# An fp32 transformer encoder on one core: layer 0's last expert added to x by products instead of a scatter

## The chip, the cores and the metric

The program runs on one core of a Trainium2 chip. The metric is the device time of one execution in microseconds (us), the median over runs. Five engines have instruction streams of their own and meet only at semaphores: TensorE (PE, matrix products into PSUM), VectorE (DVE), ScalarE (ACT), GpSimd (POOL) and SyncE (SP, which here only issues DMAs). An engine's instructions run in the order in which they are written.

## What is computed

Two request groups (256 prompt tokens and 512 sample tokens, 768 rows of 1024 numbers in all) pass through two layers. Each layer is an attention mixer and then an expert layer:

```python
for i in range(DEPTH):
    h = rms_norm(x, norm_mix[i])
    x = x + (dilated_attention(h, ...) if i % 2 == 0 else local_gqa_attention(h, ...))
    h = rms_norm(x, norm_ffn[i])
    x = x + expert_choice_ffn(h, moe_router[i], moe_w_gate[i], moe_w_up[i], moe_w_down[i])

def expert_choice_ffn(h, w_router, w_gate, w_up, w_down):
    affinity = softmax(tokens @ w_router)            # 16 experts
    gate, idx = top_k(affinity.T, cap)               # each expert takes its best tokens
    xe = tokens[idx]
    hid = silu(xe @ w_gate) * (xe @ w_up)
    ye = (hid @ w_down) * gate[..., None]
    return zeros_like(tokens).at[idx].add(ye)
```

An expert takes 64 sample tokens and 32 prompt tokens: 96 slots. All is in fp32.

## The kernel before

The 768 rows are six tiles of 128 rows. `x` in SBUF holds them. Weight products are split by hand: a weight tile `w` becomes `w_hi` (rounded, written by ScalarE) and `w_lo = w - w_hi` (VectorE), the rows likewise, and three products of the fast reduced type replace one fp32 product. In the expert layer a piece of 256 weight rows (1 MB) is loaded by SP into a ring of six, split by ScalarE and VectorE and used by TensorE. `PIECE` is the order of the 192 pieces of a layer; gate, up and down of 16 experts.

`y[:, e % 2]` holds the weighted output of expert `e` (`take_y`, ScalarE). The POOL function `add_rows` scatters it by an indirect DMA that adds to the rows of the DRAM tensor `x_d` at the expert's tokens (`take[:, e]`); each scatter waits for the one before (`rows_added`). `x_d` was stored from `x` ahead of the experts.

**The boundary between the layers.** When expert 15's scatter has landed, SP loads the six tiles of `x` back from `x_d` (line 613); ahead of that it has issued the loads of the first two attention weight chunks (`load_chunk`, line 547), as soon as the last piece is used. Layer 1 then begins, with one order per engine, written out by hand:

- ScalarE: `high_chunk(first)` (the rounded half of the first weight chunk, line 789), then `sum_of_squares` of tiles 0 and 1 (line 762), then for each tile `take_transposed` (the rounded half of the transposed rows, line 771) with the sum of squares of the tile two ahead, and `take_tile` (the product out of PSUM, line 796) of the tile before. After tile 1's it makes the rounded half of the second chunk.
- VectorE: `low_chunk(first)` (line 1082), `row_means` (line 1096), then for each tile `scale_row` (line 1101: the row times its inverse norm times the gain), `row_means` of the next tile and `low_rows` (line 1088, the low half of the transposed rows) of the tile before; after tile 3's `low_rows(2)` the low half of the second chunk.
- POOL: the inverse root of each tile's mean square (line 694), one small instruction per tile.
- TensorE: sixty `idle_products` (line 1441, a 128x128 product of the identity whose result nobody reads), then `turn_rows`: for each tile eight transposes (line 1453), and behind them `project` of the tile before (lines 1487 to 1489, 24 products with the first weight chunk). `project` of tile t waits for `low_rows(t)`.

The loop in which TensorE runs through the tiles ends as follows:

```python
for t in range(NT):
    pe.wait_ge(h_ready, n + 1)
    ...                       # eight transposes of tile t
    if then is not None and t >= 1:
        then(t - 1)           # project(first, [t - 1])
```

Here "tile t's product" means these 24 instructions. Below, `first` is `FIRST_CHUNK[1]`.

Of the kernel before, what the change touches and what calls it, by code (L numbers as in the profile page):

```python
# [36 lines left out]
ALU = mybir.AluOpType  # L37
AX = mybir.AxisListType

P = 128  # L40
BANK = 512
DM = 1024
# [5 lines left out]
LAYERS = 2  # L48
# [62 lines left out]
def shape_constants():  # L111

    buckets = np.zeros((BUCKETS + 1, TABW), np.float32)
    for start, width, half, stride, every in TAB.values():
        for i in range(width):
            rel = i - (BAND - P - 1 if width > 2 * P else P - 1)
            if rel % every == 0 and abs(rel) // every <= half:
                buckets[t5_bucket(np.array(rel * stride)), start + i] = 1.0
            else:
                buckets[BUCKETS, start + i] = MASKED  # L120
    return {"c_buckets": buckets, "c_ident": np.eye(P, dtype=np.float32)}

# [39 lines left out]
def build_trunk(nc, d, outs):  # L162

    ctx = ExitStack()
    with ctx:
        def sb(name, shape, dt=F32, scope=ctx):
            return scope.enter_context(nc.sbuf_tensor(name, shape, dt))
# [37 lines left out]
        weight = sb("weight", [C, NE])  # L205
        take = sb("take", [C, NE], I32)
        take_s = sb("take_s", [CS, NE], I32)
        take_p = sb("take_p", [CP, NE], I32)
# [128 lines left out]
        weight_ready = sem("weight_ready")  # L337

        piece_in = [sem(f"piece_in{i}") for i in range(RAW)]
        hi_split = sem("hi_split")  # L340
# [18 lines left out]

        STREAM = [slice(PT_, NT), slice(0, PT_)]  # L360

        def down_bank(e):
# [177 lines left out]
        def _(sp):  # L540
# [61 lines left out]
            for layer in range(LAYERS):  # L602
                first = FIRST_CHUNK[layer]
                chunk = first
                if layer == 0:
                    chunk = 4
                else:
                    load_chunk(first)
                    load_chunk(first + 1)
                    chunk = first + 2  # L610
                    sp.wait_ge(rows_added, 16 * NE)
                    for t in range(NT):
                        sp.dma_start(x[:, t, :], x_d[t * P:(t + 1) * P, :]).then_inc(x_in[t], 16)
                load_bias(layer, 0)
                load_bias(layer, 1)
# [61 lines left out]
                if layer + 1 < LAYERS:  # L677
                    sp.dma_start(gain[:], bass.AP(d["norm_mix"].tensor, (layer + 1) * DM, [[0, P], [1, DM]])).then_inc(gain_in, 16)
                for n in range(layer * LAYER_PIECES + SPLIT, (layer + 1) * LAYER_PIECES):
                    load_piece(n)  # L680
            sp.wait_ge(x_out, 16 * NT * LAYERS)
            sp.wait_ge(rows_added, 16 * NE * LAYERS)
            sp.wait_ge(prompt_added, 16 * NE)
# [3 lines left out]
        def _(pool):  # L687
            hnorms = 0
            for layer in range(LAYERS):
# [21 lines left out]
                def add_rows(e):  # L711

                    n = layer * NE + e
                    pool.wait_ge(y_ready, n + 1)
                    if e == 0:
# [27 lines left out]
        def _(act):  # L743
            turned = 0
            lots = 0
            for layer in range(LAYERS):
                def sum_of_squares(step, i):
# [7 lines left out]
                    else:  # L755
                        act.wait_ge(x_in[t], 16 * (layer + 1))
                        scratch = ps[:, 4:6, :].rearrange("p b n -> p (b n)")
                    if n >= 1:
# [38 lines left out]

                if layer == 0:
                    sum_of_squares(0, 0)
                    sum_of_squares(0, 1)  # L800
                high_chunk(FIRST_CHUNK[layer])
                if layer:
                    sum_of_squares(2 * layer, 0)
                    sum_of_squares(2 * layer, 1)

# [219 lines left out]
                def take_y(e, n):  # L1025
# [3 lines left out]
                    if u >= 2:  # L1029
                        act.wait_ge(rows_added, 16 * (u - 1))  # L1030
                    if layer and e >= 2:
# [30 lines left out]
        def _(dve):  # L1062
# [13 lines left out]
            for layer in range(LAYERS):  # L1076
# [25 lines left out]


                gains += 1
                if layer:
                    low_chunk(FIRST_CHUNK[layer])
                row_means(2 * layer, 0)
                row_means(2 * layer, 1)
                dve.wait_ge(gain_in, 16 * gains)
                for t in range(NT):  # L1110
                    if t >= 2:
                        dve.wait_ge(h_turned, NT * 2 * layer + t - 1)
                    scale_row(2 * layer, t, t, rows[:, t % 2, :])
                    if t == 1 and layer == 0:
                        low_chunk(FIRST_CHUNK[layer])
# [268 lines left out]
                nc.vector.tensor_copy(take_s[:], ps[0:CS, 5, 0:NE])  # L1384
                nc.vector.tensor_copy(take_p[:], ps[0:CP, 5, 32:48])
                nc.vector.tensor_copy(weight[0:CS, :], ps[0:CS, 5, 64:64 + NE])
                nc.vector.tensor_copy(weight[CS:C, :], ps[CS:C, 5, 96:96 + NE]).then_inc(weight_ready, 1)
# [27 lines left out]
                for i, (kind, e, part) in enumerate(PIECE):  # L1415
# [11 lines left out]
                    if i + SPLIT < LAYER_PIECES:  # L1427
                        split(n + SPLIT)


        @block.tensor
        def _(pe):
# [5 lines left out]
            def idle_products(count, bank=6):  # L1438

                for i in range(count):  # L1440
                    nc.tensor.matmul(ps[:, bank, 0:P], ident[:], ident[:], start=True, stop=True)  # L1441

            for layer in range(LAYERS):
                def turn_rows(s, src, then=None):
                    for t in range(NT):
                        n = NT * s + t
                        pe.wait_ge(h_ready, n + 1)
# [45 lines left out]
                if layer:  # L1493
                    idle_products(60)
                turn_rows(2 * layer, lambda t: rows[:, t % 2, :], lambda t: project(FIRST_CHUNK[layer], [t]))
# [341 lines left out]
```

## Time and profile before

| | us |
|---|---|
| median of 3 runs | 1850.18 |
| lowest and highest of them | 1849.69, 1852.94 |
| the profiled execution's own time | 1845.36 |
| its span, first to last instruction | 1843.5 |
| TensorE busy in the span | 1766.0 (96%) |
| VectorE, ScalarE, POOL busy | 1330.8, 1132.1, 238.4 |
| TensorE's share of the chain that ended last | 88% |

All times inside the trace count from the start of the span. The profiled execution is one of its own, 4.8 us below the median of the runs, so differences are worked out against it. The boundary between the layers lies at 946 us. The experts of layer 0 fill 390 to 946 us, those of layer 1 begin at 1276 us.

### The profile page before, as it was taken

What the parts mean: (1) busy time and instruction counts of PE and PEld (TensorE: products, weight loads), DVE (VectorE), ACT (ScalarE), POOL (GpSimd) and SP (SyncE); (2) the same over time, 40 slices, a digit from 0 to 9 for tenths busy, and PEclk for the clock granted to TensorE, in tenths of its full rate; (3) what the DMA queues carried; (4) which work ended last, traced back from release to release, by engine and by line L of the source; (5) the groups of instructions that cost most, each with busy time, mean ns of one, the idle gap of its engine ahead of it and who ended that gap; (6) DMA issues with size and microseconds to landing.
All of it is one profiled execution on the core that took longest, in us unless ns stands there. A gap on an engine that the chain in (4) does not pass through costs nothing.

```text
span 1843.5 us, 24587 instructions
## 1 busy us (share of the span) xinstructions
PE 1766.0 (96%) x10322; PEld 1393.7 (76%) x10322; DVE 1330.8 (72%) x1008; ACT 1132.1 (61%) x1185; POOL 238.4 (13%) x118
## 2 busy tenths in 40 slices
PE   6989999989999999999999989998999999999997
PEld 6878889977776776776779977997767767777775
DVE  4634455578888888888845556557888888888885
ACT  4344443357777777777743556434777777777774
POOL 0201000000010010010011100001111311311311
PEclk9999998999999999999999989999999999999999
DMA  4401113399999999999954012229999999999994
GB/s 159 113 30 53 44 51 108 144 354 370 389 376 384 391 380 383 394 382 383 390 181 105 18 36 56 80 97 344 361 382 392 380 384 389 375 384 393 382 389 142
DMA packets 155842, 486.00 MB, mean 264 GB/s; under 512 B 12200, under 2 KB 46120, under 8 KB 155688
## 3 DMA queue, kind: packets, MB, share of 16 engines
q1 hardware_dynamic: 148308, 459.26, 66.6%
q0 software_dynamic: 7424, 25.17, 5.8%
q8 instruction: 82, 1.34, 0.3%
q14 instruction: 28, 0.22, 0.0%
HBM read 454.26 MB, written 30.13 MB: 263 GB/s over the span
## 4 chain that ended last, share of the span: by engine, by line
PE 88%; DVE 5%; ACT 3%; DMA 2%; issue 1%; POOL 1%; SPq 0%; POOLq 0%; DVEq 0%; ACTq 0%
PE ps L1789 19%; PE ps L1791 19%; PE ps L1790 19%; PE ps L1487 5%; PE ps L1488 4%; PE ps L1489 4%; PE ps L1567 2%; PE ps L1679 2%; PE ps L1681 2%; PE ps L1680 2%; PE ps L1760 1%; PE ps L1539 1%; PE ps L1441 1%; PE ps L1753 1%; PE ps L1556 1%
## 5 line engine op out<-in xcount | busy, mean ns | idle before, releaser
L1296 DVE TENSOR_TENSOR w_lo<-ring,w_hi 128x2048 fp32r<-128x2048 f32 x384 | 876.7, 2290 | 153.1 <-ACT w_hi L1001 152.9
L1001 ACT ACTIVATE w_hi<-ring 128x2048 fp32r<-128x2048 f32 x384 | 735.9, 1917 | 276.7 <-PE ps L1791 268.4
L1789 PE MATMUL ps<-w_hi,xe_hi 128*96 128x512 f32 x1016 | 403.5, 397 | 0.0
L1791 PE MATMUL ps<-w_hi,xe_lo 128*96 128x512 f32 x1016 | 399.2, 393 | 0.0
L1790 PE MATMUL ps<-w_lo,xe_hi 128*96 128x512 f32 x1016 | 398.1, 392 | 0.0
L1791 PEld LDWEIGHTS ps<-w_hi,xe_lo 128*96 128x96 f32 x1016 | 163.9, 161 | 71.5
L1789 PEld LDWEIGHTS ps<-w_hi,xe_hi 128*96 128x96 f32 x1016 | 163.7, 161 | 69.5 <-DVE xe_lo L1395 5.6
L1790 PEld LDWEIGHTS ps<-w_lo,xe_hi 128*96 128x96 f32 x1016 | 164.3, 162 | 64.5
L1789 PE MATMUL ps<-w_hi,hid_hi 128*96 128x512 f32 x512 | 201.6, 394 | 0.0
L1791 PE MATMUL ps<-w_hi,hid_lo 128*96 128x512 f32 x512 | 201.1, 393 | 0.0
L1487 PE MATMUL ps<-c_hi,hT_hi 128*128 128x256 f32 x648 | 191.4, 295 | 9.6 <-issue 3.4
L1790 PE MATMUL ps<-w_lo,hid_hi 128*96 128x512 f32 x512 | 200.3, 391 | 0.0
L1488 PE MATMUL ps<-c_lo,hT_hi 128*128 128x256 f32 x648 | 186.9, 288 | 0.0
L1489 PE MATMUL ps<-c_hi,hT_lo 128*128 128x256 f32 x648 | 186.7, 288 | 0.0
L1487 PEld LDWEIGHTS ps<-c_hi,hT_hi 128*128 128x128 f32 x648 | 128.1, 198 | 16.0 <-issue 14.8
L1488 PEld LDWEIGHTS ps<-c_lo,hT_hi 128*128 128x128 f32 x648 | 128.4, 198 | 0.0
L1489 PEld LDWEIGHTS ps<-c_hi,hT_lo 128*128 128x128 f32 x648 | 128.3, 198 | 0.0
L1791 PEld LDWEIGHTS ps<-w_hi,hid_lo 128*96 128x96 f32 x512 | 82.5, 161 | 36.1
L1790 PEld LDWEIGHTS ps<-w_lo,hid_hi 128*96 128x96 f32 x512 | 82.7, 162 | 35.6
L1789 PEld LDWEIGHTS ps<-w_hi,hid_hi 128*96 128x96 f32 x512 | 82.5, 161 | 34.9
L720 POOL DMA_INDIRECT layer_rows<-y,take x16 | 36.8, 2302 | 492.1 <-ACT y L1034 492.1
L1237 DVE SCALAR_TENSOR_TENSOR probs<-ps,bias 128x512 f32<-128x512 f32 (+2 forms) x30 | 34.6, 1153 | 89.3 <-PE ps L1539 89.3
(190 smaller groups left out, 2255.1 us busy)
## 6 DMA issues: line engine op xcount, KB each, us to landing
ring<-in_moe_w_gate SPq DMA_DIRECT2D x128, 1024.0 KB, 7.2
ring<-in_moe_w_up SPq DMA_DIRECT2D x128, 1024.0 KB, 8.5
ring<-in_moe_w_down SPq DMA_DIRECT2D x128, 1024.0 KB, 8.6
wbuf<-in_a_w_in SPq DMA_DIRECT2D x9, 1024.0 KB, 5.5
ffn_rows<-hrow SPq DMA_DIRECT2D x12, 512.0 KB, 2.7
wbuf<-in_b_w_in SPq DMA_DIRECT2D x5, 1024.0 KB, 8.2
unit_rows<-row SPq DMA_DIRECT2D x36, 132.0 KB, 1.8
bias<-bias_rows SPq DMA_DIRECT2D x4, 768.0 KB, 10.1
```

Source lines behind the costliest of these rows:

```text
L1001: nc.scalar.activation(w_hi[:, n % SPLIT], ring[:, n % RAW], ACT.Copy).then_inc(hi_split, 1)
L1296: nc.vector.tensor_tensor(w_lo[:, n % SPLIT], ring[:, n % RAW], w_hi[:, n % SPLIT].bitcast(F32), ALU.subtract).then_inc(lo_split, 1)
L1487: nc.tensor.matmul(out, hi, c_hi[:, w, k, :], start=(k == (KM - 1 if folding else 0)), stop=False)
L1488: nc.tensor.matmul(out, hi, c_lo[:, w, k, :], start=False, stop=False)
L1489: ins = nc.tensor.matmul(out, lo, c_hi[:, w, k, :], start=False, stop=(k == (0 if folding else KM - 1)))
L1567: ins = nc.tensor.matmul(u_bank[:, h * HD:(h + 1) * HD], probsT[:, (lots + i) % 2, m * P:(m + 1) * P], v[:, g % 2 if layer == 0 else 0, k, ...
L1679: nc.tensor.matmul(out, hi, of_hi[:, k, :], start=(k == 0), stop=False)
L1680: nc.tensor.matmul(out, hi, of_lo[:, k, :], start=False, stop=False)
L1681: ins = nc.tensor.matmul(out, lo, of_hi[:, k, :], start=False, stop=(k == KX - 1))
L1789: nc.tensor.matmul(out, hi[:, k, :], w_hi[:, n % SPLIT, i, cols], start=(k == 0), stop=False)
L1790: nc.tensor.matmul(out, hi[:, k, :], w_lo[:, n % SPLIT, i, cols], start=False, stop=False)
L1791: ins = nc.tensor.matmul(out, lo[:, k, :], w_hi[:, n % SPLIT, i, cols], start=False, stop=(k == KM - 1))
```

## The change

Expert 15 of layer 0 is scattered no more. A row of the numbers 0 to 767 (`c_tokens`) is loaded during layer 0's experts, and VectorE compares it with the token of each of the expert's 96 slots (`last_slot`): `slot_tokens` is a matrix of 96 x 768 with a 1 where a slot holds a token. For each tile TensorE multiplies 128 columns of it with `y` (96 x 1024) in two fp32 products of 512 columns (`last_expert`), and VectorE adds the two PSUM banks to the tile of `x` (`add_last`). SP loads `x` when expert 14's scatter has landed; the first weight chunk is loaded behind tile 1, the second behind tile 5. The sums of squares of the first two tiles go ahead of the first chunk's rounded half, VectorE's `low_chunk(first)` goes behind `scale_row(1)`, and 14 idle products stand where 60 stood. The products of tiles 0 to 3 stand ahead of these, those of tiles 4 and 5 inside `turn_rows`.

```diff
+        slot_tokens = hrow[0:C, NT - 1, 0:TOK]
+        token_row = x[0:C, 0, 0:TOK]
+        LAST_BANK = (4, 2, 4, 2, 4, 4)
+        def rows_before(layer, e):
+            return e if layer == 0 else NE - 1 + e
...
-                    load_chunk(first)
-                    load_chunk(first + 1)
                     chunk = first + 2
-                    sp.wait_ge(rows_added, 16 * NE)
+                    sp.wait_ge(slots_marked, 1)
+                    sp.wait_ge(rows_added, 16 * (NE - 1))
                     for t in range(NT):
                         sp.dma_start(x[:, t, :], x_d[t * P:(t + 1) * P, :]).then_inc(x_in[t], 16)
+                        if t == 1:
+                            load_chunk(first)
+                    load_chunk(first + 1)
...
                 for n in range(layer * LAYER_PIECES + SPLIT, (layer + 1) * LAYER_PIECES):
+                    if layer == 0 and n == LAYER_PIECES // 2:
+                        sp.wait_ge(weight_ready, 1)
+                        sp.wait_ge(x_out, 16 * NT)
+                        sp.dma_start(token_row, bass.AP(d["c_tokens"].tensor, 0, [[0, C], [1, TOK]])).then_inc(tokens_in, 16)
                     load_piece(n)
...
+                    n = rows_before(layer, e)
+                    if layer == 0 and e == NE - 1:
+                        return
...
-                        act.wait_ge(x_in[t], 16 * (layer + 1))
-                        scratch = ps[:, 4:6, :].rearrange("p b n -> p (b n)")
+                        if layer:
+                            act.wait_ge(last_added, t + 1)
+                            scratch = qraw[:, :, :].rearrange("p t c -> p (t c)")[:, 0:DM]
...
-                if layer == 0:
-                    sum_of_squares(0, 0)
-                    sum_of_squares(0, 1)
+                sum_of_squares(2 * layer, 0)
+                sum_of_squares(2 * layer, 1)
                 high_chunk(FIRST_CHUNK[layer])
-                if layer:
-                    sum_of_squares(2 * layer, 0)
-                    sum_of_squares(2 * layer, 1)
...
+                def add_last(t):
+                    dve.wait_ge(x_in[t], 32)
+                    dve.wait_ge(last_rows, t + 1)
+                    b = LAST_BANK[t]
+                    nc.vector.tensor_tensor(x[:, t, :], ps[:, b:b + 2, :].rearrange("p b n -> p (b n)"), x[:, t, :],
+                                            ALU.add).then_inc(last_added, 1)
                 if layer:
-                    low_chunk(FIRST_CHUNK[layer])
+                    add_last(0)
+                    add_last(1)
                 row_means(2 * layer, 0)
+                if layer:
+                    add_last(2)
                 row_means(2 * layer, 1)
...
                     scale_row(2 * layer, t, t, rows[:, t % 2, :])
-                    if t == 1 and layer == 0:
+                    if layer and t + 3 < NT:
+                        add_last(t + 3)
+                    if t == 1:
                         low_chunk(FIRST_CHUNK[layer])
                     if 1 <= t < NT - 1:
                         row_means(2 * layer, t + 1)
                     if t >= 1:
                         low_rows(t - 1)
...
+                if layer == 0:
+                    nc.vector.tensor_scalar(last_slot[0:CS, :], ps[0:CS, 5, NE - 1:NE], float(SEQ), None, ALU.add)
+                    nc.vector.tensor_copy(last_slot[CS:C, :], ps[CS:C, 5, 32 + NE - 1:32 + NE])
...
+                    if layer == 0 and kind == "down" and part == 0 and e == NE - 3:
+                        dve.wait_ge(tokens_in, 16)
+                        nc.vector.tensor_scalar(slot_tokens, token_row, last_slot[:], None, ALU.is_equal).then_inc(slots_marked, 1)
...
+            def last_expert(t):
+                if t == 0:
+                    pe.wait_ge(slots_marked, 1)
+                if t >= 2:
+                    pe.wait_ge(last_added, t - 1 if t < NT - 1 else t)
+                for half in range(2):
+                    ins = nc.tensor.matmul(ps[:, LAST_BANK[t] + half, :], slot_tokens[:, t * P:(t + 1) * P],
+                                           y[:, (NE - 1) % 2, half * BANK:(half + 1) * BANK], start=True, stop=True)
+                ins.then_inc(last_rows, 1)
...
                     for t in range(NT):
+                        if s == 2 and 1 <= t < NT - 3:
+                            last_expert(t + 3)
...
                 if layer:
-                    idle_products(60)
+                    for t in range(4):
+                        last_expert(t)
+                    idle_products(14)
```

## Rows read from the trace of the kernel before

**Rows 1.** Chain of waits at the layer boundary: start us, length us, what.

```profile
946.08 1.12 ACT y L1034
...
947.46 8.34 DMA layer_rows<-y,take
955.82 0.34 SPq L613
956.21 4.60 DMA x<-layer_rows
...
963.83 1.30 DVE v L1101
...
970.70 0.87 PE ps L1453 x8
...
974.77 1.91 ACT c_hi L789
...
978.91 1.28 DVE v L1101
...
981.53 0.36 PE ps L1487
```

**Rows 2.** Timeline of TensorE: start, length, line, shapes, count, idle before.

```profile
947.24 13.66 PE L1441 MATMUL ps<-ident 128*128 128x128 f32 x120 [1.20 <-ACT y L1034]
...
967.00 0.55 PE L1487 MATMUL ps<-c_hi,hT_hi 128*128 128x256 f32 x1
...
971.33 0.36 PE L1487 MATMUL ps<-c_hi,hT_hi 128*128 128x256 f32 x1
...
974.29 1.03 PE L1453 MATMUL ps<-ident,v 128*128 128x128 f32 x8
```

**Rows 3.** Timelines of POOL, SyncE and VectorE, columns as above.

```profile
938.25 2.35 POOL L720 DMA_INDIRECT layer_rows<-y,take  x1 [44.37 <-ACT y L1034]
...
946.13 0.99 SPq L547 DMA_DIRECT2D wbuf<-in_b_w_in  x2
...
968.23 1.23 DVE L1088 TENSOR_TENSOR hT_lo<-ps,hT_hi 128x1024 fp32r<-128x1024 f32 x1
...
976.70 2.29 DVE L1082 TENSOR_TENSOR c_lo<-wbuf,c_hi 128x2048 fp32r<-128x2048 f32 x1 [2.37 <-ACT c_hi L789]
```

**Rows 4.** Issue to landing: expert 14's scatter, the six x loads, weight loads.

```profile
DMA to landing us min/median/max: 6.4/6.4/6.4
...
DMA to landing us min/median/max: 3.7/5.8/7.6
...
DMA to landing us min/median/max: 5.5/9.4/10.7
```

**Rows 5.** Instructions by line: fp32 products of 512 columns, the add from PSUM.

```profile
44.45 3.60 PE L1499 MATMUL ps<-bias,row 33*12 33x512 f32 x8
...
L1499 PE MATMUL ps<-bias,row x8: 589/589/597, 44.5 to 47.5; 33*12 33x512 f32 x8
...
L1284 DVE TENSOR_TENSOR x<-ps,x x12: 1224/1225/1226, 301.6 to 1248.0; 128x1024 f32<-128x1024 f32 x12
```

**Rows 6.** Windows of 1 us: busy time by engine, PEclk, DMA share, GB/s.

```profile
965.00:966.00 1.00, 0.83 (x4) 0.84 (x5) 0.55 (x3) 1.00 (x2) 0.55 (x1) 0.50 1.05 327
...
968.00:969.00 1.00, 1.00 (x9) 1.00 (x9) 0.88 (x3) 0.20 (x1) 0.55 (x1) 0.82 0.98 131
978.00:979.00 1.00, 0.20 (x2) 0.00 (x0) 1.00 (x2) 0.90 (x2) 0.00 (x0) 1.00 0.00 0
982.00:983.00 1.00, 1.00 (x8) 1.00 (x7) 1.00 (x2) 0.40 (x1) 0.00 (x0) 0.50 0.00 0
```

**Rows 7.** Who waits for whom in layer 0's experts; first gather before them.

```profile
ACT w_hi L1001 <- PE ps L1791: 133.2, 155, 1.5
DVE w_lo L1296 <- ACT w_hi L1001: 72.4, 138, 1.8
...
388.20 0.85 PE L1753 MATMUL ps<-ident,xg 96*128 96x96 f32 x8 [0.74 <-DMA xg<-ffn_rows,take]
```

More of the change, by code:

```diff
@@ L120, in shape_constants @@
                 buckets[BUCKETS, start + i] = MASKED
-    return {"c_buckets": buckets, "c_ident": np.eye(P, dtype=np.float32)}
+    return {"c_buckets": buckets, "c_ident": np.eye(P, dtype=np.float32),
+            "c_tokens": np.arange(TOK, dtype=np.float32)[None, :]}
 def units_of(layer):
@@ L206, in build_trunk @@
         take = sb("take", [C, NE], I32)
+        last_slot = sb("last_slot", [C, 1])
         take_s = sb("take_s", [CS, NE], I32)
@@ L337, in build_trunk @@
         weight_ready = sem("weight_ready")
+        tokens_in = sem("tokens_in")
+        slots_marked = sem("slots_marked")
+        last_rows = sem("last_rows")
+        last_added = sem("last_added")
         piece_in = [sem(f"piece_in{i}") for i in range(RAW)]
@@ L679, in _ @@
                 for n in range(layer * LAYER_PIECES + SPLIT, (layer + 1) * LAYER_PIECES):
+                    if layer == 0 and n == LAYER_PIECES // 2:
+                        sp.wait_ge(weight_ready, 1)
+                        sp.wait_ge(x_out, 16 * NT)
+                        sp.dma_start(token_row, bass.AP(d["c_tokens"].tensor, 0, [[0, C], [1, TOK]])).then_inc(tokens_in, 16)
                     load_piece(n)
             sp.wait_ge(x_out, 16 * NT * LAYERS)
-            sp.wait_ge(rows_added, 16 * NE * LAYERS)
+            sp.wait_ge(rows_added, 16 * rows_before(1, NE))
             sp.wait_ge(prompt_added, 16 * NE)
@@ L711, in add_rows @@
                 def add_rows(e):
-                    n = layer * NE + e
-                    pool.wait_ge(y_ready, n + 1)
+                    n = rows_before(layer, e)
+                    if layer == 0 and e == NE - 1:
+                        return
+                    pool.wait_ge(y_ready, layer * NE + e + 1)
                     if e == 0:
@@ L755, in sum_of_squares @@
                     else:
-                        act.wait_ge(x_in[t], 16 * (layer + 1))
-                        scratch = ps[:, 4:6, :].rearrange("p b n -> p (b n)")
+                        if layer:
+                            act.wait_ge(last_added, t + 1)
+                            scratch = qraw[:, :, :].rearrange("p t c -> p (t c)")[:, 0:DM]
+                        else:
+                            act.wait_ge(x_in[t], 16)
+                            scratch = ps[:, 4:6, :].rearrange("p b n -> p (b n)")
                     if n >= 1:
@@ L1029, in take_y @@
                     if u >= 2:
-                        act.wait_ge(rows_added, 16 * (u - 1))
+                        act.wait_ge(rows_added, 16 * (rows_before(layer, max(e - 1, 0))))
                     if layer and e >= 2:
```

## The prediction

> **What bounds the kernel now.** I read the page's engine shares first, then the chain of waits, then the engines' timelines around the one place that the change touches. TensorE is busy for 96% of the span and carries 88% of the chain. In layer 0's experts ScalarE waits for TensorE to free a split buffer, 133.2 us in total and never for a load, and VectorE for ScalarE [rows 7]: TensorE sets the pace there, and the other engines and the loads have room. At 946 us the chain leaves TensorE: ScalarE takes expert 15's output, the scatter needs 8.34 us, the reload of x 4.60 us from issue to the second tile, then sums, inverse roots and scaling [rows 1]. TensorE meanwhile runs its 60 idle products, 13.66 us [rows 2], transposes tile 0 at 963.4 and starts tile 0's product at 967.0. A second detour follows: tile 1's product ends at 974.29 [rows 2], ScalarE then makes the second chunk's rounded half, VectorE its low half, and only behind that scales tile 4, so that tile 3's product starts at 981.53 [rows 1]. From there to 1010 us TensorE is the chain, so what counts is how much earlier or later tile 3's product starts.
>
> **What can be had.** Expert 14's scatter was issued at 938.25 [rows 3] and landed 6.4 us later [rows 4], at 944.65, ahead of the last product. So the reload need not wait for expert 15, and the 8.34 us of its scatter leave the path. In exchange come twelve fp32 products, six adds and the first chunk's low half, which was hidden behind the scatter. I follow the new order engine by engine; a wait costs 0.05 us.
>
> **Step 1, the products of tiles 0 to 3.** The nearest rows of an fp32 product of 512 columns are line 1499's: each product is recorded as two, eight take 3.60 us and one alone 0.589, so a further one costs (3.60 - 0.59) / 7 = 0.43 us [rows 5]. A tile (two products, four records) costs 1.72 us, and 0.16 more until VectorE may read. The first starts when y is there, at 947.24, as the idle products did [rows 2]. x tile 0, issued at 944.7, lands 3.7 us later [rows 4], at 948.4. The six tiles landed between 959.5 (955.8 + 3.7) and 965.9 (958.3 + 7.6), one each 1.27 us, so tile 1 lands at 949.6. Both adds, 1.225 us each [rows 5], are done at 950.4 and 952.1, just ahead of the products of tiles 2 and 3 that reuse their banks. So TensorE runs through: 947.24 + 4 x 1.72 = 954.1. Fourteen idle products at 13.66 / 60 = 0.228 us bring it to 957.3.
>
> **Step 2, the first transposes.** The first chunk is issued at 946.13 as before [rows 3] but lies behind tiles 0 and 1; with 2.5 to 3 us for its 1 MB at the rate of x it lands at 952.5, and tiles 2 to 5 at 954.0, 955.3, 956.6 and 957.9. Add 2 ends at 955.3, tile 1's mean follows, and tile 0 is scaled (1.28 us) by 956.6. That is 0.7 us ahead of the end of the idle products: the transposes start at 957.3 instead of 963.4. 6.1 us are gained here.
>
> **Step 3, what is given back before tile 0's product.** Transposes 0.87 us [rows 1], to 958.2. Then TensorE has tile 4's products: to 959.9, readable at 960.1. VectorE has added tile 3 and scaled tile 1 by 958.9 and waits for them: add 4 to 961.3, then the first chunk's low half, 2.29 us [rows 3], to 963.6, then tile 0's low rows, 1.23 us [rows 3], to 964.8. Tile 0's product starts at 964.85 instead of 967.0: 2.15 us are left.
>
> **Step 4, the clock.** In the kernel before TensorE idled from 960.9 to 963.4, and the granted clock was 0.50 (1.2 GHz) from about 965 until some way into the 968 window, where it reads 0.82 [rows 6]: 3.3 us. The next idle stretch, 978.2 to 980.25, brought 0.50 at 982 [rows 6]. Now TensorE idles from 960.9 to 964.85, longer than either. I charge the stretch of about 3.2 us at 0.50 that both rows show, beginning with the product: 1.6 us of work are lost. At full clock a tile's product takes 24 x 0.12 = 2.9 us (971.33 to 974.29 with its hand-over [rows 2]), so it ends at 969.4.
>
> **Step 5, tile 5 stands in front of tile 1's product.** TensorE's order is now tile 0's product, tile 5's products, transposes 2, tile 1's product. Tile 5's are readable at 969.4 + 1.72 + 0.16 = 971.2. VectorE scaled tile 2 by 966.1 and stands at add 5 since; queued behind it are tile 3's mean and tile 1's low rows, for which tile 1's product waits. Add 5 ends at 972.4, the low rows at 973.7. In the kernel before these low rows were made at 968.23 [rows 3] and nobody waited. Tile 1's product starts at 973.75 instead of 971.33: 2.4 us later.
>
> **Step 6, the rest of the path.** The second detour hangs on the end of tile 1's product and moves with it: ScalarE's rounded half at 977.1 instead of 974.77, VectorE's low half (2.29 us), tile 4's scaling, transposes, tile 3's low rows; tile 3's product starts at 983.8 instead of 981.53. With the same idle stretch in front of it comes the same half clock behind it. Sum: 1.7 + 0.2 (tile 5's products) + 1.2 (its add) + 1.2 (the low rows behind it) + 0.2 of waits, less 2.15 gained, and 0.0 from the clock since tile 0's product loses what it lost before to within 0.3: between 2.2 and 2.4, I take **+2.3 us**. The same working on the old order gives 981.5 for tile 3's product, as the trace has it.
>
> **Edits costed at nothing.** The token row (0.3 MB) goes through SP's queue in the middle of the experts; ScalarE never waits for a piece there [rows 7], with weight loads of 1 MB landing in 5.5 to 10.7 us elsewhere [rows 4]; uncovered it would cost 0.8 us, its size at the rate of x. The comparison (96 x 768, bounded from above by the 1.225 us of a 1024-column add [rows 5]) falls into VectorE's waits for ScalarE, 72.4 us in 138 of them [rows 7]; uncovered 1.2 us, once. The two copies for `last_slot` delay the splits of the first pieces by 0.3 us while TensorE waits for the first gather until 388.20 [rows 7]. The missing scatter frees POOL, which is idle anyway. From below all these are nothing; none can gain.
>
> **Rivals.**
> *The clock falls once more, or for longer.* Step 5 opens a new idle stretch, 972.0 to 973.75, between the 1.2 us ahead of the idle products, after which these ran at their full rate [rows 2], and the 2.05 us that cost the clock [rows 6]. If it falls in tile 1's product, this ends 1.0 us later, tile 3's product starts 1.2 later, and what TensorE gains on its later half clock leaves +3.0; if the first low stretch covers all of tile 0's product, 1.1 us more: +4.1. [...] Chance 0.2.
> *x comes late: slower.* Tiles 2 to 5 lie behind a weight chunk now. One of the two chunks took 10.7 us to land [rows 4]; if the first does so here (956.8), tile 2 lands at 958.1 instead of 954.0. From 954.7 on each us of lateness is one of time: +5.7. Slower by over 0.2% from a landing of 956.1 on. For it speaks that six tiles and two chunks now share one stretch; against it that 10.7 belonged to the second chunk, beside a scatter. Chance 0.15, with expert 14's scatter needing more than 6.4 us.
> *The clock stays up: no loss.* If the dense products ahead keep it at full rate through both idle stretches, tile 0's product takes 2.9 us and tile 3's runs at full rate: 1.6 + 1.6 us less, **-0.9 us**. Against it stand both low stretches of before. To get past 0.2% faster it needs cheaper products too: at 0.23 us per record (the rate of the reduced products is the floor I allow) the sum would be -3.0. Chance 0.12.
>
> **How the numbers follow.** The sum stands against the profiled execution's 1845.36 us: 1847.7. The median of the runs is 4.8 us higher; the difference carries over, 1850.18 + 2.3 = 1852.5 us. 0.2%, about what a measurement of this kernel tells from no change, is 3.7 us. The sum has 0.53, with a range of its own from +0.7 to +3.6. Below it the range reaches to the case of -0.9, with 1.3 for the spread of runs: 1848.0; above to late x and the spread: 1857. Slower by over 0.2%: late x (0.15), half of the clock's case (0.1), a little of the sum: 0.27. Faster: 0.07 from the case of a full clock. Within 0.2%: 0.66.
>
> **What would show it.** Right: SP's first x load near 944.7; last idle product near 957; tile 0's product 2 us earlier, tile 1's 2 to 3 us later than before; VectorE's longest waits before adds 4 and 5, for TensorE; the low clock in tile 0's product. Wrong: tile 1's low rows done before tile 5's add; an add that waits for a load; records of the new products far from 0.43 us apart; PEclk at 1.00 throughout.

## The result and the profile after

The changed kernel is a little slower: its median is 1854.18 us in ten runs (1850.38 to 1857.8), beside 1849.19 us in ten runs of the kernel before (1844.2 to 1852.94). The ratio is 1.0028 with a 95% interval of 1.0017 to 1.0039: 5.2 us more, between 3.1 and 7.2. A second measurement (e7) gave 1.0023 (1.0014 to 1.0033), 4.3 us. The forecast was +2.3 us, 1852.5 (1848 to 1857). The sign and the place were right; the size was about half of what was measured. Times given as "measured" are medians; the ratios stand against the kernel before, run beside. One run of the twelve of experiment e8 took 7668.78 us and is left out of its figures.

The two profiled executions differ by about as much, 1850.38 against 1845.36 us, but for the most part not at the place of the change. I set marks: the start of ScalarE's instruction that takes expert 15's output `y`, and the start of the one that takes the product of the boundary's last tile, tile 5 (ScalarE's timelines, before and after):

```profile
992.80 0.38 ACT L796 ACTIVATE kraw<-ps 128x256 f32<-128x256 f32 x1 [2.50 <-PE ps L1489]
```

```profile
992.61 0.38 ACT L824 ACTIVATE kraw<-ps 128x256 f32<-128x256 f32 x1 [2.50 <-PE ps L1546]
```

`y` is taken at 946.08 and 944.76 us in these two traces. From mark to mark ("the boundary" from here on) the kernel before took 46.72 us and the changed one 47.85: of the 5.1 us between the spans 1.1 lie here. The eighteen units of layer 1's attention took 120.22 and then 124.04 us, though nothing was changed in them.

The chain of waits of the changed kernel at the boundary (start, length, what) answers to [rows 1].

```profile
944.76 1.12 ACT y L1058
945.93 7.13 PE ps L1494 x16
953.06 3.13 PE ps L1485 x28
956.18 1.01 PE ps L1510 x8
957.20 1.73 PE ps L1494 x4
959.02 1.22 DVE x L1133
960.25 2.20 DVE c_lo L1106
962.51 1.14 DVE hT_lo L1112
...
968.25 1.73 PE ps L1494 x4
970.08 1.23 DVE x L1133
971.36 1.14 DVE hT_lo L1112
...
976.06 1.92 ACT c_hi L817
...
980.21 1.28 DVE v L1125
```

The scatter and the reload of x are gone from the chain, as the change intends. In their place stand sixteen records of the new products (L1494), the idle products, then tile 4's products, their add (L1133), the first chunk's low half (L1106) and tile 0's low rows (L1112); later tile 5's products, their add and tile 1's low rows. The second detour, from ScalarE's `c_hi` at 976.06 on, stands as it was.

The timeline of VectorE (start, length, line, what, idle time before and who ended it), beside [rows 3]:

```profile
953.57 1.22 DVE L1133 TENSOR_TENSOR x<-ps,x 128x1024 f32<-128x1024 f32 x1 [2.55 <-DMA x<-layer_rows]
...
959.02 1.22 DVE L1133 TENSOR_TENSOR x<-ps,x 128x1024 f32<-128x1024 f32 x1 [0.65 <-PE ps L1494]
...
970.08 1.23 DVE L1133 TENSOR_TENSOR x<-ps,x 128x1024 f32<-128x1024 f32 x1 [5.24 <-PE ps L1494]
971.22 0.14 DVE L1120 TENSOR_SCALAR var<-sumsq 128x1 f32<-128x1 f32 x1
971.28 1.22 DVE L1112 TENSOR_TENSOR hT_lo<-ps,hT_hi 128x1024 fp32r<-128x1024 f32 x1
```

VectorE stands 5.24 us at the add of tile 5 for TensorE's products, with tile 1's low rows behind it. TensorE in turn stands for those low rows. Its timeline, beside [rows 2]:

```profile
945.93 7.13 PE L1494 MATMUL ps<-y,hrow 96*128 96x512 f32 x16 [1.20 <-ACT y L1058]
...
963.79 0.55 PE L1544 MATMUL ps<-c_hi,hT_hi 128*128 128x256 f32 x1 [4.00 <-DVE hT_lo L1112]
...
972.64 0.36 PE L1544 MATMUL ps<-c_hi,hT_hi 128*128 128x256 f32 x1 [1.79 <-DVE hT_lo L1112]
...
981.55 1.09 PE L1510 MATMUL ps<-ident,v 128*128 128x128 f32 x8 [2.06 <-DVE v L1125]
```

Both new idle stretches are there, 4.00 us ahead of tile 0's product and 1.79 us ahead of tile 1's, and the old one of 2.06 us ahead of tile 4's transposes, which stand in front of tile 3's product. The windows of 1 us (the number behind the five engines is PEclk, TensorE's granted clock) show one low stretch in this execution, that is one run of windows at 0.50, the lower of the clock's two levels, in tile 0's product, where [rows 6] have two:

```profile
963.00:964.00 1.00, 0.21 (x1) 0.24 (x2) 1.00 (x2) 0.00 (x0) 0.14 (x1) 0.72 1.18 141
964.00:965.00 1.00, 1.00 (x6) 1.00 (x7) 0.83 (x1) 0.00 (x0) 0.00 (x0) 0.50 0.86 129
...
966.00:967.00 1.00, 1.00 (x7) 1.00 (x6) 0.00 (x0) 0.00 (x0) 0.00 (x0) 0.57 0.95 131
967.00:968.00 1.00, 1.00 (x11) 1.00 (x10) 0.00 (x0) 0.00 (x0) 0.00 (x0) 1.00 0.88 101
...
983.00:984.00 1.00, 1.00 (x10) 1.00 (x10) 1.00 (x2) 0.70 (x1) 0.00 (x0) 1.00 0.00 0
```

### The profile page after: what moved, and what is told of

Its sections match the earlier page's. It is cut to its first block, busy times and chain, and to the rows that moved or that the text cites. A ratio compares the mean times of both kernels' runs of the same rounds, so it can differ in the third digit from the quotient of the medians.

```text
span 1848.6 us, 24468 instructions
## 1 busy us (share of the span) xinstructions
PE 1764.6 (95%) x10254; PEld 1385.7 (75%) x10254; DVE 1338.2 (72%) x1017; ACT 1132.3 (61%) x1185; POOL 237.2 (13%) x117
## 4 chain that ended last, share of the span: by engine, by line
PE 88%; DVE 5%; ACT 3%; DMA 2%; issue 1%; POOL 1%; SPq 0%; POOLq 0%; DVEq 0%; ACTq 0%
PE ps L1848 19%; PE ps L1850 19%; PE ps L1849 19%; PE ps L1544 5%; PE ps L1546 4%; PE ps L1545 4%; PE ps L1626 2%; PE ps L1738 2%; PE ps L1740 2%; PE ps L1739 2%; PE ps L1598 2%; PE ps L1819 1%; PE ps L1485 1%; PE ps L1812 1%; PE ps L1615 1%
```

## The experiments

e1 to e4 ran on one chip, e5 to e8 on a second, the four single runs e9 to e12 on a third. The medians of the kernel before were 1850.55 us (35 runs) on the first and 1848.75 us (34 runs) on the second.

### e1: the kernel before once more

No edit. The question is whether low clock in layer 1's attention belongs to the change.

> The kernel before once more, for the granted clock of its single runs and a second trace. Theory A: the change costs about 2.6 us at the layer boundary (tile 3's product 2.6 us later after expert 15's output), and the rest of the measured 5 us is stretches of half clock elsewhere that come and go between executions of either kernel: then the mean granted clock of these runs scatters from 0.980 to 0.988 as that of the changed kernel does, and the new trace has low stretches at places where the first had none. Theory B: the change itself brings low stretches to layer 1 (at 1131 us and ahead of layer 1's experts, 4.5 us in the first trace): then these runs stay near 0.988 and the new trace has full clock at both places.

Measured: 1848.92 us, ratio 0.999 (0.9977 to 1.0004); the profiled span was 1850.5 us, 7.0 us longer than the first trace of the very same kernel. Layer 1's attention took 125.27 us instead of 120.22. The windows that cover it exactly, first of the first trace, then of this one:

```profile
1054.85:1175.07 120.22, 109.66 (x841) 94.25 (x839) 67.49 (x70) 68.78 (x205) 8.33 (x2) 0.96 0.19 53
```

```profile
1055.20:1180.47 125.27, 113.06 (x841) 96.24 (x839) 67.55 (x70) 68.55 (x205) 8.33 (x2) 0.93 0.19 51
...
981.00:982.00 1.00, 1.00 (x7) 1.00 (x8) 1.00 (x1) 0.00 (x0) 0.55 (x1) 0.69 0.00 0
982.00:983.00 1.00, 1.00 (x6) 0.96 (x5) 1.00 (x2) 0.38 (x1) 0.00 (x0) 0.50 0.00 0
```

The same 841 matmul records run at a mean granted clock of 0.93 instead of 0.96, and TensorE is busy for 3.4 us longer with them. So what the two first traces differ by in layer 1 is no work of the change: the first trace of before was the luckiest of all fourteen there (the others took 121.9 to 126.6 us). Theory B falls; the mean granted clock of these runs, too, scatters from 0.981 to 0.989, as Theory A had it. The last two lines are from the boundary: this execution has only the second of the low stretches of [rows 6], at tile 3's product, and its boundary is 45.52 us, 1.2 shorter than in the first trace.

### e2: the preparations alone

The kernel before with the token row, `last_slot` and the comparison, whose result nobody uses:

```diff
+                        sp.dma_start(token_row, bass.AP(d["c_tokens"].tensor, 0, [[0, C], [1, TOK]])).then_inc(tokens_in, 16)
...
+                    nc.vector.tensor_scalar(last_slot[0:CS, :], ps[0:CS, 5, NE - 1:NE], float(SEQ), None, ALU.add)
+                    nc.vector.tensor_copy(last_slot[CS:C, :], ps[CS:C, 5, 32 + NE - 1:32 + NE])
...
+                        nc.vector.tensor_scalar(slot_tokens, token_row, last_slot[:], None, ALU.is_equal).then_inc(slots_marked, 1)
```

> The kernel before with layer 0's part of the change alone: token row, slot tokens and the comparison are made but not used; scatter, reload and layer 1 are as before. By the working in which these edits cost nothing: 0 us, within 1.5 us. Rival: they are the unexplained part of the loss, 2 to 3 us slower, with a TensorE wait near the comparison in expert 13 or ahead of the first gather.

Measured: 1851.48 us, ratio 0.9999 (0.9985 to 1.0012). From the first expert's output to the sixteenth's layer 0 took 508.16 us, beside 508.11 in the first trace of before. The comparison itself took 0.61 us and nobody waited for it (the instruction's own view):

```profile
L1447 DVE TENSOR_SCALAR hrow<-x,last_slot x1: 610/610/610, 883.6 to 883.6; 96x768 f32<-96x768 f32 x1
```

These edits cost nothing, as the forecast had it.

### e3: tile 5's products ahead of tile 1's transposes

Tile 5 gets banks of its own, so that its products can go directly behind tile 4's, ahead of tile 0's product:

```diff
-        LAST_BANK = (4, 2, 4, 2, 4, 4)
+        LAST_BANK = (4, 2, 4, 2, 6, 4)
...
-                    pe.wait_ge(last_added, t - 1 if t < NT - 1 else t)
+                    pe.wait_ge(last_added, min(t - 1, 3))
...
-                        if s == 2 and 1 <= t < NT - 3:
-                            last_expert(t + 3)
+                        if s == 2 and t == 1:
+                            last_expert(4)
+                            last_expert(5)
```

> The changed kernel with tile 4's products in banks 6 and 7 and tile 5's right behind them, ahead of tile 1's transposes, so that nothing stands between tile 0's and tile 1's product but the transposes of tile 2. If step 5 is what loses the gain: counted from expert 15's output, tile 0's product starts as in the changed kernel (19.0 us), tile 1's starts 24.5 us after it instead of 27.9 (26.6 in the kernel before was 25.25), and the time falls by 3.4 us against the changed kernel, to about 1 us below the kernel before by the boundary alone. If instead the clock or layer 0's edits make the loss, tile 1's product moves as said but the time stays 4 to 5 us above the kernel before.

(A bracket in this text is garbled: the start of tile 1's product in the kernel before, counted from `y`, is 971.33 - 946.08 = 25.25 us [rows 1, 2].)

Measured: 1849.78 us, ratio 0.9999 (0.9988 to 1.0009). The whole loss is gone. VectorE's timeline shows how:

```profile
964.79 1.22 DVE L1133 TENSOR_TENSOR x<-ps,x 128x1024 f32<-128x1024 f32 x1
...
965.99 1.21 DVE L1112 TENSOR_TENSOR hT_lo<-ps,hT_hi 128x1024 fp32r<-128x1024 f32 x1
...
974.38 2.29 DVE L1106 TENSOR_TENSOR c_lo<-wbuf,c_hi 128x2048 fp32r<-128x2048 f32 x1 [2.37 <-ACT c_hi L817]
```

The add of tile 5 waits for nobody, tile 1's low rows are done at 967.2, before tile 0's product ends, and tile 1's product is taken 27.76 us after `y` instead of 31.02 in the changed kernel. The boundary is 44.58 us, 3.3 us below the first trace of the changed kernel, which lost as much to the clock (table below); 3.4 us were expected. So step 5 is what eats the gain.

### e4: the first idle stretch filled

Seventeen idle products between tile 1's transposes and tile 0's product:

```diff
                        ins.then_inc(h_turned, 1)
+                        if s == 2 and t == 1:
+                            idle_products(17)
```

> The changed kernel with 17 idle products between tile 1's transposes and tile 0's product, where TensorE idled 4.0 us. If the low clock in tile 0's product comes from that gap: PEclk 1.00 there, the product takes 2.9 us instead of 4.4, and the time falls by 1.5 us against the changed kernel, still 2 to 3.5 us above the kernel before. If the low stretch has another cause, the product keeps its 4.4 us and the time does not change.

Measured: 1852.6 us, ratio 1.0014 (1.0002 to 1.0027). TensorE now waits for 0.20 us instead of 4.00, and the clock stays up (timeline, then two of the windows):

```profile
960.94 3.96 PE L1485 MATMUL ps<-ident 128*128 128x128 f32 x34
965.10 0.36 PE L1546 MATMUL ps<-c_hi,hT_hi 128*128 128x256 f32 x1 [0.20 <-DVE hT_lo L1112]
...
966.00:967.00 1.00, 1.00 (x11) 1.00 (x10) 0.15 (x1) 0.00 (x0) 0.00 (x0) 1.00 0.94 121
967.00:968.00 1.00, 1.00 (x11) 1.00 (x10) 0.00 (x0) 0.00 (x0) 0.00 (x0) 1.00 0.99 129
```

Tile 0's product is taken 22.02 us after `y` instead of 23.53: the 1.5 us that step 4 charged to the clock. Then a low stretch appears at tile 3's product, which the first trace of the changed kernel did not have, and the boundary comes out at 47.48. One portion of clock was saved, another was paid elsewhere; 1.79 us of waiting ahead of tile 1's product remain. The timed ratio, beside 1.0028 and 1.0023 of the changed kernel with overlapping intervals, is too coarse to show a gain of 1.5 us.

### e5: the reload alone, without the products

No products and no adds, so expert 15's rows of layer 0 are left out; 36 idle products keep TensorE busy instead:

```diff
-                            act.wait_ge(last_added, t + 1)
+                            act.wait_ge(x_in[t], 32)
...
                     dve.wait_ge(x_in[t], 32)
-                    dve.wait_ge(last_rows, t + 1)
...
+                    return
...
-                        if s == 2 and 1 <= t < NT - 3:
-                            last_expert(t + 3)
...
-                    for t in range(4):
-                        last_expert(t)
-                    idle_products(14)
+                    idle_products(36)
```

> The changed kernel without the twelve products and six adds (expert 15's rows of layer 0 are left out), 36 idle products in place of 14. It prices what the early load of x is worth when nothing has to be added. By the steps: counted from expert 15's output, tile 0's product starts at 12.6 us (kernel before 20.9, changed kernel 19.0), tile 5's product is taken at about 38 us (before 45.4 to 46.7, changed 47.9), and the time is 8 to 9 us below the kernel before: the products and adds then take back 10 us. Rival: the reload is not what bounds the boundary, and the time falls by less than 4 us.

Measured: 1844.6 us, ratio 0.9973 (0.9964 to 0.9982), 5.0 us (3.3 to 6.7) faster than before, not 8 to 9. The interval alone does not exclude the rival's 4 us; the boundary, 40.42 us, is 5.0 to 6.3 us shorter than in any trace of the kernel before. The trace shows where the rest went. The mean of tile 1 stands in VectorE's order behind tile 2's wait for x, which I had left in (VectorE's timeline, then TensorE's):

```profile
956.48 0.15 DVE L1120 TENSOR_SCALAR var<-sumsq 128x1 f32<-128x1 f32 x1 [6.24 <-DMA x<-layer_rows]
956.93 2.48 DVE L1125 SCALAR_TENSOR_TENSOR v<-x,rstd,gain 128x1024 f32<-128x1024 f32 x2 [0.29 <-issue]
...
958.27 3.45 PE L1505 MATMUL ps<-ident,v 128*128 128x128 f32 x16 [2.57 <-DVE v L1125]
```

Tile 2 landed 10.2 us after `y` (946.23 in this trace), beside 8.4 to 8.8 in the four traces of the changed kernel, where VectorE waits for it too, but TensorE's products and idle products last longer. TensorE idled for 2.57 us, the clock fell to 0.50 in the transposes (3.45 us for two tiles that take 2 x 0.87 at full clock), and tile 0's product started at 16.72 instead of 12.6. The miss is my wait and the late load. Why the load landed later here I can't say.

### e6: a new order

All that e3 showed, and the first chunk behind tile 2 of x. ScalarE's and VectorE's orders are written out (a: add of the last expert, m: mean, s: scaling, c: a chunk's half, l: low rows; q: sum of squares, h: taking a transposed tile, k: taking a product; the digit is the tile, or the chunk). Tile 0's product still waits for the fifth add:

```diff
+        LAST_BANK = (4, 2, 4, 2, 6, 4)
+        ACT_ORDER = order("q0 q1 c0 h0 q2 q3 h1 q4 k0 h2 k1 q5 h3 c1 h4 k2 k3 h5 k4 k5")
+        DVE_ORDER = order("a0 a1 m0 a2 m1 s0 s1 c0 a3 l0 a4 m2 l1 m3 m4 s2 s3 a5 l2 s4 m5 l3 s5 l4 c1 l5")
...
-                        if t == 1:
+                        if t == 2:
                             load_chunk(first)
...
+                        if s == 2 and t == 1:
+                            last_expert(4)
+                            last_expert(5)
+                            pe.wait_ge(last_added, 4)
...
+                        if s == 2 and t == 1:
+                            pe.wait_ge(last_added, 5)
...
-                    idle_products(14)
+                    idle_products(4)
```

> The change with another order in layer 1's first stretch: tiles 4 and 5 multiplied behind tile 0's transposes (banks 6 and 4), the first chunk loaded behind tile 2, rows of tiles 0 and 1 scaled ahead of the adds of tiles 3 to 5, low rows ahead of the adds that nobody waits for, the second chunk's halves made late. If the loss was only the order in which the adds and products stand: tile 0's product starts 16.0 us after expert 15's output (changed kernel 19.0, before 20.9), tile 1's 19.8 (27.9, 25.3), tile 5's is taken at 36.9 (47.9, 45.4 to 46.7), no low clock in between, and the time is 8 to 9 us below the kernel before. If the fp32 products themselves are too dear whatever their place: not below the kernel before by more than 3 us.

Measured: 1844.54 us, ratio 0.997 (0.9958 to 0.9983): by the ratio 5.5 us faster than the kernel before (by the medians 4.2), and by the medians 8.7 us faster than the changed kernel beside it (e7), the fastest of the kernels that leave nothing out. 8 to 9 us against the kernel before were expected. The boundary is 39.05 us. The rows show the third add, the start of tile 0's product and the transposes of tiles 4 and 5:

```profile
953.07 1.23 DVE L1154 TENSOR_TENSOR x<-ps,x 128x1024 f32<-128x1024 f32 x1 [0.43 <-PE ps L1525]
...
962.92 0.39 PE L1579 MATMUL ps<-c_hi,hT_hi 128*128 128x256 f32 x1 [1.17 <-DVE x L1154]
...
974.87 1.04 PE L1543 MATMUL ps<-ident,v 128*128 128x128 f32 x8
...
978.61 1.04 PE L1543 MATMUL ps<-ident,v 128*128 128x128 f32 x8
```

No add waits for a load, and tile 0's product starts 16.5 us after `y` (946.38) instead of 19.0. That is 0.5 us later than expected, and the product still ran through a low stretch (taken 4.67 us after its start, in e4 at full clock 3.14), so the boundary came out 2.1 us above the expected 36.9.

Not all of this undoes step 5. Of the 5.5 us between this boundary and e3's, 2.9 come ahead of tile 0's product (16.54 us after `y` against 19.43). Most of the rest is the second detour: the second chunk's halves are made late (c1), so TensorE no longer stands for 2 us ahead of tile 4's transposes. The kernel before has that detour too and could have been spared it; no run tried this, so what e6 gains over the kernel before is not the price of the change in a good order alone.

### e7: the changed kernel once more

No edit.

> The changed kernel once more, on the same chip as the others, for a second interval and a second trace. By the sum of steps 1 to 6: 2.3 us above the kernel before, with tile 5's product taken 47 to 49 us after expert 15's output. Rival (something outside the boundary adds to it): 4 us or more above, at the same boundary.

Measured: 1853.19 us, ratio 1.0023 (1.0014 to 1.0033). Its boundary took 49.73 us instead of 47.85. Both are above what was expected (2.3 us over the kernel before, a boundary of 47 to 49), and the rival does not fit either, as it kept the boundary as it was. The windows show a low stretch that begins ahead of tile 0's product and lasts through all of it, and later a second one:

```profile
964.00:965.00 1.00, 0.00 (x0) 0.00 (x0) 1.00 (x3) 0.00 (x0) 0.00 (x0) 0.62 0.97 144
...
970.00:971.00 1.00, 1.00 (x7) 1.00 (x6) 0.00 (x0) 0.00 (x0) 0.00 (x0) 0.50 0.94 141
971.00:972.00 1.00, 1.00 (x6) 0.71 (x5) 0.00 (x0) 0.48 (x2) 0.00 (x0) 0.97 0.72 91
...
985.00:986.00 1.00, 1.00 (x6) 1.00 (x6) 1.00 (x2) 0.00 (x0) 0.42 (x1) 0.50 0.00 0
```

### e8: the first chunk's low half ahead of the fourth add

```diff
+                    if t == (0 if layer else 1):
+                        low_chunk(FIRST_CHUNK[layer])
                     if layer and t + 3 < NT:
                         add_last(t + 3)
-                    if t == 1:
-                        low_chunk(FIRST_CHUNK[layer])
```

> The changed kernel with VectorE's low half of the first chunk moved ahead of tile 3's add, nothing else. It prices step 3's low half and leaves step 5 in place. By the working tile 0's product starts at 18.4 us after expert 15's output instead of 19.0, as the adds of tiles 3 and 4 now stand behind the low half; TensorE's idle stretch is cut in two of 2.0 and 1.5 us. If the clock then stays up, tile 1's product starts at 25.7 instead of 27.9 and the time falls by 2.1 us against the changed kernel; if not, by 0.6.

Measured: 1850.2 us, ratio 1.0013 (0.9999 to 1.0026), boundary 47.26. Tile 0's product starts 18.3 us after `y` and each product is taken 0.6 us earlier than in the first trace of the changed kernel; the clock falls as before. The timed difference to e7 (1.0023) is larger than 0.6 us, but the intervals overlap. The low half is a small part of the wait; the order of tile 5 is the large one.

### e9 to e12: four more traces, two of each kernel

No edits; e9 and e11 are the kernel before, e10 and e12 the changed one.

> One more trace of the kernel before. Where does the part of the loss sit that the boundary traces do not show (boundary +2.9 us in the mean, timed +4.1 and +4.7 us)? If in low clock at the boundary that differs from one execution to the next: from expert 15's output to tile 5's product 43.5 to 46.7 us here, so that the mean of the traces of before falls below 45.9. If it sits in layer 1's attention: 66 to 149 us later stages shorter here than in the changed kernel.

> As the other look at the kernel before: boundary 43.5 to 46.7 us, attention of layer 1 between 120 and 127 us.

> One more trace of the changed kernel: from expert 15's output to tile 5's product 47.9 to 49.7 us as in its two traces (before 45.4 to 46.7); the attention of layer 1 between 120 and 127 us as in every kernel. If the unexplained part is in the attention, this stretch is at its long end here each time.

> As the other look at the changed kernel: boundary 47.9 to 49.7 us, attention of layer 1 between 120 and 127 us.

Measured: 1851.84 and 1848.94 us for the kernel before, 1851.29 and 1853.35 for the changed one; one more run of the kernel before beside them took 1843.27, so single runs decide nothing. Their boundaries are what counts. With all earlier traces they make this table, whose second column adds up 1 - PEclk over the windows of 1 us from `y` to 52 us behind it: the full-speed work that the low clock took away.

| kernel, trace | boundary us | lost to the clock us |
|---|---|---|
| before, first trace | 46.72 | 3.4 |
| e1 | 45.52 | 1.7 |
| e2 (before with the preparations) | 45.39 | 1.7 |
| e9 | 45.58 | 1.7 |
| e11 | 46.34 | 3.4 |
| after, first trace | 47.85 | 1.7 |
| e7 | 49.73 | 5.1 |
| e10 | 50.65 | 5.1 |
| e12 | 49.62 | 5.1 |
| e3 tile 5 early | 44.58 | 1.7 |
| e4 gap filled | 47.48 | 1.7 |
| e8 chunk ahead | 47.26 | 1.7 |
| e5 no products | 40.42 | 1.7 |
| e6 new order | 39.05 | 1.7 |

In e10 the second of three low stretches lies in tile 1's product, right behind the new idle stretch of 1.79 us:

```profile
972.00:973.00 1.00, 0.37 (x3) 0.40 (x4) 1.00 (x2) 0.00 (x0) 0.00 (x0) 1.00 0.00 0
973.00:974.00 1.00, 1.00 (x10) 1.00 (x10) 1.00 (x3) 0.00 (x0) 0.18 (x1) 0.93 0.00 0
974.00:975.00 1.00, 1.00 (x7) 1.00 (x7) 0.87 (x1) 0.00 (x0) 0.36 (x1) 0.50 0.00 0
```

The five traces with the boundary of before have a mean of 45.91 us, the four of the changed kernel 49.46: +3.55 us, inside both timed intervals. Traces with the same loss to the clock, one portion of 1.7 us, give 47.85 against a mean of 45.50: **+2.35 us**, the forecast, though on the side of the changed kernel this is a single trace. The rest, 3.55 - 2.35 = 1.2 us, is by this count the clock: the four traces lost 4.3 us to it on average, the five 2.4, and part of that difference of 1.9 falls where TensorE idles anyway.

Two expectations are answered by this, one of them with a miss. The mean of the traces of before did not fall below 45.9; it is the changed kernel that came out longer, e10 with 50.65 us above the 47.9 to 49.7 that were expected. And the missing part does not sit in layer 1's attention, which took 121.97 and 123.69 us in e10 and e12, 125.26 and 123.32 in e9 and e11. Outside the boundary these nine traces show no loss on average: up to `y` the means are 946.3 us before and 945.7 after, behind tile 5's product 855.9 and 855.4.

## Why the prediction was right in its mechanism and too small in its size

**Step 1** held. Counted from `y`, everything came at the time forecast: sixteen records took 7.13 us, so 0.43 each with the first one's 0.59, and the last idle product ended 11.4 us after `y` (forecast 957.3 - 946.08 = 11.2). One part was off: tile 2 of x landed about 0.9 us later than forecast, VectorE's third add waited 2.55 us for it, and tile 0 was scaled at 956.04, only 0.15 us ahead of the idle products' end at 956.19. It cost nothing, by that little. "An add that waits for a load" was among the prediction's own signs of being wrong, and it came; and of VectorE's waits that were to be its longest, that ahead of add 4 was 0.65 us only.

**Step 2** held: the transposes began 11.4 us after `y` (11.2 forecast).

**Step 3** held: tile 0's product started 19.03 us after `y`, forecast 18.77, beside 20.92 before. 1.9 of the 2.15 us were left.

**Step 4** held in the first trace, with one low stretch in tile 0's product (taken at 23.53); e4, with the stretch gone, took it at 22.02, 1.5 us earlier, where 1.6 was charged. In e7 and e12 the low stretch was twice as long.

**Step 5** held, and e3 shows that it decides: tile 1's product started 27.88 us after `y` (forecast 27.67, before 25.25), VectorE waited 5.24 us at the add of tile 5, and with that add out of the way the loss was gone.

**Step 6** failed in one term, the "0.0 from the clock". The step took it that the changed kernel loses to the clock what the kernel before lost. It does in some executions and not on average: 1.7, 5.1, 5.1 and 5.1 us in four traces, beside 3.4, 1.7, 1.7, 1.7 and 3.4. The mechanical sum of the step, +2.3, came out at +2.35, so close with some luck, as it rests on one trace of the changed kernel; the clock added 1.2.

**The rivals.** *The clock falls once more, or for longer* is what most executions of the changed kernel do, and both of its forms occurred: in e10 the clock fell in tile 1's product behind the new 1.79 us, and in e7 and e12 the first low stretch covered all of tile 0's product. Its price, +3.0 to +4.1, holds the +3.55 of the means, and I had given it 0.2 against 0.53. Form by form the price fits less well. Against the first trace of before, on which the sum stands, e7 and e12 came to +3.0 and +2.9 and e10 to +3.9, where its form was priced at +3.0: the price counted on a gain at the later low stretch, and in e10 that one cost its 1.7 us like the others. The trace of before had two low stretches behind two gaps, and I read that as what always happens; e1, e2 and e9, with one each, show it was one draw. *x comes late* was near, not decisive: the point from which it decides was 956.1 - 946.08 = 10.0 us after `y`, and tile 2 came at 8.4 to 8.8 in the changed kernel and at 10.2 in e5, which paid for it. *The clock stays up* occurred in none of the traces.

The edits that the forecast costed at nothing cost nothing (e2).

**The chances.** The prediction gave 0.66 to a change within 0.2% and 0.27 to a slower one, the latter for late x (0.15), half of the case in which the clock falls (0.1) and a little of the sum; of these it was the clock. Both measured ratios, 0.28% and 0.23%, lie just beyond 0.2%, with 0.2% inside both intervals. The measured 1854.18 us lies in the upper part of the stated range, which had been left there for a late x and the spread of runs, not for the clock.

Open: why the same idle stretches keep the full clock in one execution and lose it in another. All four traces of the changed kernel have 4.0 us, 1.8 us and about 2 us of idle TensorE at the same three places, and one has one low portion, three have three. With one trace each, the clock's part in e3, e4 and e8 is one draw too. The timed ratios say 5.2 and 4.3 us, the boundaries 3.55, the whole spans of the same nine traces 2.4 in the mean; single executions scatter by more than these differences, and nothing here divides them further.

## What to carry to other kernels

When work is moved to fill an idle engine, follow what stands behind it in the in-order queue of every other engine: here a 1.2 us add placed one step too early in VectorE's order, for products placed one step too late in TensorE's, gave back more than was left of the gain (1.9 us at tile 0's product became a loss of 2.6 us at tile 1's), and placing those products one tile earlier undid the loss by itself. Where a clock may fall behind a gap, a single trace is one draw: take several traces of both kernels, cut them into stages by the same marks, and compare draws of equal clock loss with one another. And look at the stages that nobody touched, before the difference of two spans is put down to the change.

## What the runs showed of the hardware that I had not expected

Executions of one and the same kernel on one core differ widely: 35 runs of the kernel before beside e1 to e4 took from 1844.92 to 1855.83 us. The spans of its first trace and of e1 differ by 7.0 us (1843.5 and 1850.5), 5.05 of them in the eighteen attention units of layer 1, where the mean granted clock was 0.96 and 0.93; these units took 120.2 to 126.6 us over the fourteen traces. At the boundary the clock takes away 1.7 us or whole multiples of it (3.4, 5.1) in every one of them.

A small POOL instruction that works on one column of 128 elements took almost three times its usual time while VectorE scaled a row beside it (POOL's timeline of the changed kernel; the scaling of tile 0 began at 954.77):

```profile
951.10 0.57 POOL L716 TENSOR_TENSOR rstd<-var,minus_half 128x1 f32<-128x1 f32 x1 [11.81 <-DVE var L1120]
954.93 1.52 POOL L716 TENSOR_TENSOR rstd<-var,minus_half 128x1 f32<-128x1 f32 x1 [3.26 <-DVE var L1120]
```

It was off the path here. In the kernel before it lay on the chain: there its second one took 1.55 us, and VectorE waited 0.44 us for it ahead of scaling tile 1.
